# Token-shift mixtures of the recurrent projections from neighbour sums with a scaled copy on ScalarE, and the first two weight panels of keys and of values multiplied together

## What is computed (the part that matters)

```python
SEQ, CTX_LEN, D_MODEL = 512, 256, 1024
def centred_shift(x):
    prev = jnp.pad(x[:, :-1], ((0, 0), (1, 0), (0, 0)))
    nxt = jnp.pad(x[:, 1:], ((0, 0), (0, 1), (0, 0)))
    return 0.5 * (prev + nxt) - x

def rwkv_features(h, mu, wr, wk, wv, w0, w1, w2, a0, a1, a2, g1, g2, ...):
    xx = centred_shift(h)
    mix = lambda j: h + xx * mu[j]
    xw, xk, xv, xa = mix(1), mix(2), mix(3), mix(4)
    k = xk @ wk
    v = heads(xv @ wv)
    ...  # per direction d: tanh(xw @ w1[d]), xa @ a1[d]
    r = heads(mix(0) @ wr)
    g = jax.nn.sigmoid(mix(5) @ g1) @ g2
```

## Time and profile before

| what | value |
|---|---|
| device time, median of 3 runs | 2886.74 us (2886.58 to 2891.61) |
| profiled execution, its span | 2897.4 us |
| TensorE, VectorE, ScalarE busy, share of the span | 92%, 62%, 40% |
| mean granted TensorE clock | 0.962 |
| the stage, first panel of r to the end of a1 | 954.75 to about 1200 us |

### The profile page before, as it was taken

One profiled execution on the slowest core, in us unless ns is written; L12 is line 12 of the kernel. 1 busy time (PEld: TensorE's weight loads), 2 busy tenths in 40 slices (PEclk: granted clock), 3 DMA queues, 4 the chain that ended last, 5 costly groups with the idle time before them and its releaser, 6 DMA issues. The chain is left out here.

```text
span 2897.4 us, 66810 instructions
## 1 busy us (share of the span) xinstructions
PE 2672.9 (92%) x29488; PEld 2330.1 (80%) x29488; DVE 1802.8 (62%) x2834; ACT 1163.5 (40%) x1813; POOL 34.3 (1%) x46
## 2 busy tenths in 40 slices
PE   8999989999998799688888888899998999999998
PEld 4977989999998598577777776788887776788887
DVE  6656875655545645468888865755657545566632
ACT  5226443222223533345555534433324447444421
POOL 0011000000000000000000000000000000000000
PEclk9999989999998899899999998899999999999999
DMA  7320224334432222310010003455542120222332
GB/s 265 129 90 29 89 91 130 124 121 131 131 99 85 82 96 78 125 33 26 27 32 27 27 11 128 138 189 174 181 131 71 39 78 2 80 88 95 102 93 82
DMA packets 90083, 271.63 MB, mean 94 GB/s; under 512 B 9587, under 2 KB 14835, under 8 KB 89717
## 3 DMA queue, kind: packets, MB, share of 16 engines
q1 hardware_dynamic: 85236, 257.67, 26.9%
q10 hardware_dynamic: 4608, 10.49, 1.0%
HBM read 251.60 MB, written 16.52 MB: 93 GB/s over the span
## 5 line engine op out<-in xcount | busy, mean ns | idle before, releaser
L508 DVE TENSOR_TENSOR weights_low<-raw_weights,weights_high 128x1024 fp32r<-128x1024 f32 (+4 forms) x328 | 351.5, 1072 | 679.4 <-ACT weights_high L471 678.6
L471 ACT ACTIVATE weights_high<-raw_weights 128x1024 fp32r<-128x1024 f32 (+4 forms) x328 | 306.5, 935 | 932.6 <-PE psum L243 897.9
L243 PE MATMUL psum<-mlp_in_high,weights_high 128*128 128x512 f32 (+1 forms) x1104 | 363.3, 367 | 7.8 <-ACT pool_u L1068 5.1
L243 PE MATMUL psum<-mlp_in_high,weights_low 128*128 128x512 f32 (+1 forms) x1104 | 361.8, 365 | 0.0
L243 PE MATMUL psum<-mlp_in_low,weights_high 128*128 128x512 f32 (+1 forms) x1104 | 357.6, 365 | 0.7 <-DVE mlp_in_low L1050 0.5
L243 PEld LDWEIGHTS psum<-mlp_in_high,weights_high 128*128 128x128 f32 x1104 | 204.4, 189 | 34.9 <-issue 5.6
L243 PE MATMUL psum<-hidden_high,weights_low 128*128 128x384 f32 (+1 forms) x768 | 229.5, 352 | 0.0
L243 PE MATMUL psum<-hidden_high,weights_high 128*128 128x384 f32 (+1 forms) x768 | 229.5, 352 | 0.0
L243 PE MATMUL psum<-hidden_low,weights_high 128*128 128x384 f32 (+1 forms) x768 | 229.4, 352 | 0.0
L243 PEld LDWEIGHTS psum<-mlp_in_low,weights_high 128*128 128x128 f32 x1104 | 203.9, 188 | 25.2 <-DVE mlp_in_low L1050 1.9
L243 PEld LDWEIGHTS psum<-mlp_in_high,weights_low 128*128 128x128 f32 x1104 | 204.8, 189 | 22.6
(11 more groups left out here) (543 smaller groups left out, 5252.5 us busy)
## 6 DMA issues: line engine op xcount, KB each, us to landing
raw_weights<-in_mlp_w SPq DMA_DIRECT2D x96, 512.0 KB, 4.4
mod_space<-in_ada SPq DMA_DIRECT2D x56, 512.0 KB, 3.7
pool_u<-in_ada SPq DMA_DIRECT2D x56, 512.0 KB, 3.7
raw_weights<-in_w_up SPq DMA_DIRECT2D x44, 512.0 KB, 3.3
raw_weights<-in_mlp_w SPq DMA_DIRECT2D x64, 256.0 KB, 3.1
work<-in_ada SPq DMA_DIRECT2D x21, 512.0 KB, 5.4
raw_weights<-in_w_down SPq DMA_DIRECT2D x16, 512.0 KB, 3.5
raw_weights<-in_w_in SPq DMA_DIRECT2D x12, 512.0 KB, 4.5
```

Of the source, the lines that this page charges most:

```text
L243: last = nc.tensor.matmul(out[:, a, :] if wide else out, w[:, cols], x[:, at, t0:t1], start=first, stop=final)
L471: nc.scalar.activation(halves_of(ph, j)[0], raw_of(ph, j), ACT.Copy).then_inc(high.sem, 1)
L508: nc.vector.tensor_tensor(lo, raw_of(ph, j), hi.bitcast(F32), ALU.subtract).then_inc(split.sem, 1)
```

## The change

Turns 0 and 1 no longer use the difference. ScalarE writes (1 - mu) * h in the `full` buffer (`weigh`, a copy scaled by a column, one slab ahead of its rounding), and VectorE adds (0.5 * mu) * near to it in place. The `difference` of a slab is made in turn 2. Four more columns are made in `TokenShift`. Second, for phases of more than one panel (`together`), panels 0 and 1 are multiplied in one loop over the slabs: panel 1 follows two slabs (`LAG`) behind panel 0.

```diff
@@ class MixedPhase
+    LAG = 2
+    def two_products(self, pe, first, second, split, done):
+        for j in range(2):
+            self.open(pe, j)
+        pe.wait_ge(split.sem, self.split0 + 1)
+        for k in range(DT + self.LAG):
+            if k == self.LAG:
+                pe.wait_ge(split.sem, self.split0 + 2)
+            if k < DT:
+                pe.wait_ge(*self.mixture.fed(self.turn, k))
+                last = self.product(pe, 0, k, *first)
+                if k == DT - 1:
+                    last.then_inc(done.sem, 1)
+            if k >= self.LAG:
+                last = self.product(pe, 1, k - self.LAG, *second)
+        last.then_inc(done.sem, 1)
@@ gemm_split, TensorE
-                        pe.wait_ge(split.sem, ph.split0 + turn(ph, j) + 1)
-                        ph.products(pe, j, *halves_of(ph, j)).then_inc(done.sem, 1)
+                        if ph.together and j == 0:
+                            ph.two_products(pe, halves_of(ph, 0), halves_of(ph, 1), split, done)
+                        elif not ph.together or j > 1:
+                            pe.wait_ge(split.sem, ph.split0 + turn(ph, j) + 1)
+                            ph.products(pe, j, *halves_of(ph, j)).then_inc(done.sem, 1)
@@ TokenShift.vector
+        for i, mu in enumerate(self.later):
+            nc.vector.tensor_scalar(c[:, 4 + 2 * i, :], mu, 0.5, None, ALU.mult).then_inc(self.made.sem, 1)
+            nc.vector.tensor_scalar(c[:, 5 + 2 * i, :], mu, -1.0, 1.0, ALU.mult, ALU.add).then_inc(self.made.sem, 1)
@@ Mixture
+    SUMMED = 2
+    def weigh(self, eng, turn, k):
+        mu, dst, tokens, after = self.turns[turn]
+        n = DT * turn + k
+        if n >= 2:
+            eng.wait_ge(self.low.sem, self.low0 + n - 1)
+        self.core.nc.scalar.activation(self.full[n % 2][:, 0:tokens], self.h[:, k, 0:tokens], ACT.Copy,
+                                       scale=col(self.shift.columns[:, 5 + 2 * turn, :], k)).then_inc(self.weighed.sem, 1)
@@ Mixture.vector
-            if n < DT:
-                self.shift.difference(dve, k)
-                dve.wait_ge(self.shift.differenced.sem, self.shift.at["differenced"] + k + 1)
-            nc.vector.scalar_tensor_tensor(self.full[n % 2][:, 0:tokens], self.shift.diff[:, k, 0:tokens], col(mu, k),
-                                           self.h[:, k, 0:tokens], ALU.mult, ALU.add).then_inc(self.mixed.sem, 1)
+            if turn < self.SUMMED:
+                full = self.full[n % 2][:, 0:tokens]
+                dve.wait_ge(self.weighed.sem, self.weighed0 + n + 1)
+                nc.vector.scalar_tensor_tensor(full, self.shift.diff[:, k, 0:tokens], col(self.shift.columns[:, 4 + 2 * turn, :], k), full,
+                                               ALU.mult, ALU.add).then_inc(self.mixed.sem, 1)
+            else:
+                if turn == self.SUMMED:
+                    self.shift.difference(dve, k)
+                    dve.wait_ge(self.shift.differenced.sem, self.shift.at["differenced"] + k + 1)
+                nc.vector.scalar_tensor_tensor(self.full[n % 2][:, 0:tokens], self.shift.diff[:, k, 0:tokens], col(mu, k),
+                                               self.h[:, k, 0:tokens], ALU.mult, ALU.add).then_inc(self.mixed.sem, 1)
@@ Mixture.scalar
+            if turn < self.SUMMED:
+                if k == 0:
+                    self.weigh(eng, turn, k)
+                if k < DT - 1:
+                    self.weigh(eng, turn, k + 1)
             eng.wait_ge(self.mixed.sem, self.mixed0 + n + 1)
```

More of the change, by code:

```diff
@@ L208, in __init__ @@
         self.paired = paired or tokens > 512
-    rows = True
+    rows, together = True, False
     def begin(self, core):
@@ L272, in __init__ @@
         super().__init__(name, act, tokens, evict, nt, paired=True)
-        self.mixture, self.turn = mixture, turn
+        self.mixture, self.turn, self.together = mixture, turn, nt > 1
+    LAG = 2
     def products(self, pe, j, high, low):
@@ L1472, with __init__ @@
     SEGMENTS = ((0, SEQ), (SEQ, T0))
-    def __init__(self, core, X, root, scaling, sums, y, gains, before, tmp, mu, columns, diff, dst, spill):
+    def __init__(self, core, X, root, scaling, sums, y, gains, before, tmp, mu, columns, diff, dst, spill, later):
         super().__init__(core, T0, X, root, scaling, sums, y, gains, before, tmp)
-        self.mu, self.columns, self.diff, self.dst, self.spill = mu, columns, diff, dst, spill
+        self.mu, self.columns, self.diff, self.dst, self.spill, self.later = mu, columns, diff, dst, spill, later
         self.scaling = self
@@ L1484, in __init__ @@
         self.at = {n: counter(core, n).base for n in names}
-        for n, more in zip(names, (4, 16 * 4, DT, DT, DT, DT, DT, DT, DT)):
+        for n, more in zip(names, (8, 16 * 4, DT, DT, DT, DT, DT, DT, DT)):
             counter(core, n).base += more
@@ L1508, in scalar @@
         eng.wait_ge(self.spilled.sem, self.at["residual_spilled"] + 16 * 4)
-        eng.wait_ge(self.made.sem, self.at["shift_columns"] + 4)
+        eng.wait_ge(self.made.sem, self.at["shift_columns"] + 8)
         def high(k):
@@ L1580 @@
 class Mixture:
+    SUMMED = 2
     def __init__(self, core, shift, h, space, turns, count):
         self.core, self.shift, self.h, self.turns = core, shift, h, turns
+        self.weighed = counter(core, "mix_weighed")
+        self.weighed0 = self.weighed.base
+        self.weighed.base += DT * self.SUMMED
         self.full = [space[:, i * T0:(i + 1) * T0] for i in range(2)]
@@ L3778, in build @@
                 GS, sig = Split(core, s, "gate_split", [P, 1, SEQ]), core.sb(s, "gate_sigmoid", [P, SEQ])
-                space, shift_columns = core.sb(s, "shift_space", [P, 4 * T0]), core.sb(s, "shift_columns", [P, 4, DT])
+                space, shift_columns = core.sb(s, "shift_space", [P, 4 * T0]), core.sb(s, "shift_columns", [P, 8, DT])
                 mu = [column("rw_mu", j * DT, DT) for j in range(6)]
@@ L3786, in build @@
                 shift = TokenShift(core, X, root, scaling, sums, Y, both("out"), before,
-                                   [space[:, i * T0:(i + 1) * T0] for i in range(2)], mu[0], shift_columns, Y, M[0], dram["x"])
+                                   [space[:, i * T0:(i + 1) * T0] for i in range(2)], mu[0], shift_columns, Y, M[0], dram["x"], (mu[1], mu[2]))
                 staged = space[:, 0:2 * T0].rearrange("p (n t) -> p n t", n=2)
```

## The result

| | kernel before | changed kernel |
|---|---|---|
| median, first measurement | 2892.33 us (6 runs, 2886.58 to 2895.15) | 2922.88 us (6 runs, 2919.09 to 2924.93) |
| ratio | | 1.0092, 95% interval 1.0075 to 1.0109 |
| median, measured again | 2895.57 us (9 runs) | 2919.08 us (5 runs) |
| ratio | | 1.0076, 95% interval 1.0062 to 1.0090 |

The change makes the kernel slower. The ratios on record put it at 22 and 27 us, the medians of the table are 23.5 and 30.6 us apart; the sum had 24.5. The median of 2922.88 lies outside the range of 2904 to 2918. The base of three runs on which I put the sum, 2886.74, was low: with more runs the same kernel has 2892 to 2899.

The account below looks back on a forecast made before the run. TensorE was taken as the bound in most of the stage, VectorE where a phase takes fresh mixtures. 14.8 us at k_ plus 9.7 at v_ made 24.5, added to 2886.7: 2911.2 us, range 2904 to 2918.

Parts of the forecast that it names:

- the sum: All terms together: 14.8 us at k_ and 9.7 us at v_, 24.5 us slower.
- panel 1's weights for k_ later: Slower turn 1 (5.9 us) and its later first low part (0.25) delay the split of k_'s panel 1 weights by 6.1 us.
- six products on the path, at each place: At k_ and again at v_, 14 products and not 8 follow panel 1's weights: 6 x 1.06 = 6.4 us.
- clock at each place: Half clock on TensorE behind the idle hole at k_ and at v_ costs 2.3 us each, bounds 0 and 2.9.
- difference ahead of turn 3: In k_'s last job turn 2's difference is not hidden; turn 3 and v_'s panel 1 weights come 1.0 us later.
- k_ 2 begins later: Loss at k_: 6.1 + 6.4 + 2.3 = 14.8 us.
- g1 to v_ 2: Loss at v_: 1.0 + 6.4 + 2.3 = 9.7 us.
- the stage: The part of the program around the mixtures, forecast to take 24.5 us more.
- 2886.7 + 24.5 = 2911.2: Last step, whole kernel: the loss of 24.5 us added to the median of the runs, giving the forecast time in us.
- the runs' own spread of 5 us: Whole kernel: the allowance for variation between runs, 5 us, within the range of 2904 to 2918.
- The first rival: At k_ and v_ panel 1's weights arrive before slab 2, so the joint loop works: -3.9 us, 2882.8; chance 0.03.
- the 2.90 us a slab: Turn 1: low, copy and mixture with two hand-overs of 0.04 us chain to 2.90 us a slab against 1.92.

Follow-up runs that it names:

- e6_fill: Changed kernel with matmuls whose results nobody reads in TensorE's two holes, 80 in k_ and 50 in v_; ratio 1.0058.
- e7: Kernel before plus joint loop, panel 1's weights split behind the second slab, and unread matmuls ahead of the first two slabs; ratio 1.0004.
- e8: Kernel before with the edits of e7 and of e1 together; ratio 0.9987, median 2894.45 against 2898.89 us.
- e1: Kernel before with the tile shift_columns eight column groups wide and not four, the new ones unused; ratio 0.9994.
- e9: Changed kernel with the tile shift_columns twelve groups wide and not eight; ratio 1.0073.
- e3: Kernel before with the joint loop alone; ratio 1.0052, +15 us.

## Why the prediction was right and wrong

By its own steps, in us:

| step | forecast | measured | from |
|---|---|---|---|
| panel 1's weights for k_ later | 6.1 | 6.3 | 1043.80 against 1037.06, less 0.4 by which r began later |
| six products on the path, at each place | 6.4 | 6.2 | 6 x 1.04; the joint loop alone gives 8.5 with the clock |
| clock at each place | 2.3 | 1.9 and 2.0; 1.7 and 1.8 by filling | 3.76 and 3.9 us at 0.50; e6_fill |
| difference ahead of turn 3 | 1.0 | 1.0 | 1112.59 to 1113.58 |
| k_ 2 begins later | 14.8 | 14.2 | 105.00 - 90.84 |
| g1 to v_ 2 | 9.7 | 8.9 | 38.76 - 29.86 |
| pace of matmuls | not foreseen | -1.5 in panels 2 to 7 | 49.92 against 50.68, twice |
| g2 and a1 | 0 | +1.6 | 28.25 against 26.69; other runs 26.6 to 28.4; mostly a1's clock |
| the stage | 24.5 | 23.1 | |

The 1.6 us of g2 and a1 are mostly the clock again. The kernel before has 3.4 us of a1 at the low level, behind an idle time of 2.67 us, and the changed kernel 5.8, behind 3.10. a1 begins at 1190.01 and at 1212.38, so the first of these stretches lies 2 to 4 us behind its beginning and the second 3.6 to 5.6:

```profile
1192.00:1194.00 2.00, 2.00 (x9) 2.00 (x8) 0.00 (x0) 0.00 (x0) 0.00 (x0) 0.59 1.04 412
1216.00:1218.00 2.00, 2.00 (x8) 2.00 (x8) 0.00 (x0) 0.00 (x0) 0.00 (x0) 0.50 0.71 283
```

That the sum comes within 1.4 us of the stage is in part luck: the -1.5 of the pace and the +1.6 of g2 and a1 were both not foreseen, and cancel.

The mechanism held: nothing of panel 1 was overlapped, and the overlap of panel 0 was given up with it, since the split weights stood behind the whole of the mixtures in the written order. The run with the joint loop alone and the one with the early split show this apart from the rest. The copy is on the chain with two buffers: 2.96 us a slab against the 2.90 worked out, and the run with the copies alone shows its price. In turn 0 the start of w1 moved by 0.1 us. No wait came at panels 2 and 3.

The step that failed is the last one, "2886.7 + 24.5 = 2911.2", and the term of the range "the runs' own spread of 5 us". The base of 2886.7 measured 2892.33 and the spread of one kernel's runs 14 and 21 us (29 runs each: 2887.34 to 2901.70 and 2887.30 to 2908.01). The three runs shown had a median of 2886.74; the kernel before has 2892.33 with six runs, 2894.12 and 2898.89 with 29 each, 2895.57 with nine. I took the level of three runs for the kernel's level, although its profiled execution, with a span of 2897.4, lay 10.7 us above them, and added the difference to their median as it was. That gap was a sign that three runs had not shown the spread. Against its own base of 2892.33 the forecast would have been 2916.8. The rest to 2922.88, some 6 us, is not shown to be the change's: the same two kernels measured again are 23.5 us apart and not 30.6, and the four medians of the kernel before differ by 6.6 us. The difference of 24.5 us, a ratio of 1.0085, lies in both intervals.

Three smaller things were wrong. The first rival's -3.9 us counted four products behind the last slab and forgot that TensorE does not keep up with 2.1 us of products a slab; with early weights and the clock held up it is -3.1. I took 0.04 us for the hand-over around the copy, where the rows have 0.04 before it and 0.10 behind it (35.66 + 0.93 against 36.69), which makes the 2.90 us a slab 2.96. And I took the clock for a matter of holes. It fell after idle times of 1.6 us with the copies alone, and in the changed kernel ahead of the first hole. The kernel before could have told me, at the first two slabs of v_:

```profile
1103.94 0.59 PE L243 MATMUL psum<-mixed_high,weights_high 128*128 128x384 f32 x2 [1.88 <-DVE mixed_low L1608]
...
1105.77 1.01 PE L243 MATMUL psum<-mixed_high,weights_high 128*128 128x384 f32 x2 [0.36 <-DVE mixed_low L1608]
```

Left open: why the recurrence differs by up to 14 us between executions, why the low clock in r and in a1 lasts longer in one execution than in another, why the load of `wkv_ups` is slower in e7 and e8, and what in the address sets the pace of the matmuls. I moved all tiles behind shift_columns together, so which of them matters was not tried.

## What to carry to other kernels

Joining two panels moves the need for the second one's weights ahead; look in each engine's written order at where they are made, and move that with it. A copy taken off a busy engine gains nothing where the buffer it writes is freed by that engine's last step: count the chain around the buffers, not the engine's busy time. And base an absolute forecast on the spread of many executions, the profiled one included; a difference is worth far more than a level.

## What the runs showed of the hardware that I had not expected

- Moving tiles by 128 bytes in each partition changed the mean distance of matmuls of 384 columns from 176.0 to 173.3 ns, and by 128 more back to 176.0 (175.6 in v_); with the same instructions. In the first 800 us of the program such matmuls start 173.3 to 173.6 ns apart in the kernel before, in e1, in the changed kernel and in e9 alike. In this stage it is worth 1.8 us.
- TensorE's granted clock fell to 0.50 in a gap of 2.50 us, and in the changed kernel and the one with copies alone after idle times of 1.6 us between short work, while waits of 0.54 to 0.60 us in turn 1 of the kernel before left it at 1.00. Once it had fallen, 3.8 and 3.9 us of work passed at the low level behind the holes of 14.92 and 9.57 us, 5.1 us behind the 10.50 of e3, and 6.2 us behind the gap of 2.50: the longer hole did not cost more.
